# Picking experts for heads 2 to 7 of a prompt tile beside the next tile's first steps

## The reference, cut to what matters

```
q = (xb @ w_query).reshape(blk, 8, 2, 128)              # 8 heads, 2 halves
s = einsum('thcd,ckd->thck', q, sub_keys)               # 128 scores per half
top_s, top_i = top_k(s, 16)
cand = top_s[:, :, 0, :, None] + top_s[:, :, 1, None, :]
best_s, best_j = top_k(cand.reshape(blk, 8, 256), 16)   # 16 experts a head
idx = take_along_axis(cand_idx, best_j); gate = softmax(best_s)
act = gelu(einsum('td,thkd->thk', xb, expert_u[idx]))
out = einsum('thk,thkd->td', gate * act, expert_v[idx])
```

## Time and profile before

| | us |
|---|---|
| time, median of 3 runs | 2681.64 (2680.01 to 2682.45) |
| span of the profiled execution, first to last instruction | 2677.1 |
| TensorE matmul busy | 1865.1 (70%) |
| VectorE busy | 1581.6 (59%) |
| GpSimd busy | 1332.7 (50%) |
| ScalarE busy | 298.2 (11%) |
| moved by DMA | 859.13 MB, 320 GB/s over the span |

### The profile page before, as it was taken

The page is one execution under the profiler, slowest core; times in us unless marked ns, Lnnn a source line. Parts: engine busy times, 40 slices in busy tenths (PEclk is TensorE's granted clock), DMA queues, the critical chain, the costliest instruction groups (busy, mean ns, idle before and its releaser), DMA issues. The chain is left out here.

```text
span 2677.1 us, 23553 instructions
## 1 busy us (share of the span) xinstructions
PE 1865.1 (70%) x7672; PEld 847.1 (32%) x7672; DVE 1581.6 (59%) x3814; ACT 298.2 (11%) x682; POOL 1332.7 (50%) x1480
## 2 busy tenths in 40 slices
PE   7999889974174666677777576755656647556677
PEld 4477755851170001022333224431113422001112
DVE  2388843569998766742649648797454432833311
ACT  2133311210000000001200102100012100000000
POOL 0011521226566777755655446645555444577772
PEclk9999889987556666688898787976778878699999
DMA  4231225439999999999999999998999989999995
GB/s 147 95 126 64 86 56 188 158 112 396 400 400 409 409 409 409 410 374 401 370 405 403 358 392 361 405 402 297 397 366 352 329 316 393 376 409 409 409 408 230
DMA packets 325769, 859.13 MB, mean 321 GB/s; under 512 B 26826, under 2 KB 93338, under 8 KB 325618
## 3 DMA queue, kind: packets, MB, share of 16 engines
q0 software_dynamic: 184320, 671.17, 64.0%
q1 hardware_dynamic: 141326, 186.46, 20.0%
HBM read 845.25 MB, written 12.17 MB: 320 GB/s over the span
## 5 line engine op out<-in xcount | busy, mean ns | idle before, releaser
L2096 DVE SCALAR_TENSOR_TENSOR arena<-arena,banks 128x1024 f32<-128x1024 f32 x640 | 762.4, 1219 | 457.0 <-DMA arena<-peer_u,arena 451.2
L1070 PE MATMUL banks<-arena 128*32 128x512 f32 x2560 | 697.3, 719 | 343.5 <-DMA arena<-peer_v,arena 334.0
L2426 POOL DMA_INDIRECT arena<-peer_v,arena x640 | 609.9, 953 | 435.4 <-issue 203.4
L2426 POOL DMA_INDIRECT arena<-peer_u,arena x640 | 608.2, 950 | 405.3 <-issue 193.6
L1070 PEld LDWEIGHTS banks<-arena 128*32 128x32 f32 x2560 | 92.3, 116 | 823.2 <-DMA arena<-peer_v,arena 666.5
L863 PE MATMUL banks<-wring,uT 128*64 128x512 f32 (+3 forms) x512 | 258.5, 655 | 93.3 <-DMA wring<-w_q 35.0
L536 PE MATMUL banks<-cst,arena 128*128 128x128 f32 (+5 forms) x514 | 79.8, 304 | 177.7 <-DVE arena L1979 82.7
L863 PEld LDWEIGHTS banks<-wring,uT 128*64 128x64 f32 (+1 forms) x512 | 89.2, 184 | 267.8 <-issue 203.2
L564 PE MATMUL banks<-wring,uT 128*128 128x512 f32 (+1 forms) x320 | 142.7, 603 | 0.8 <-DVE uT L1912 0.8
L605 PE MATMUL banks<-uT,wring 128*128 128x320 f32 x512 | 139.1, 433 | 0.0
L536 PEld LDWEIGHTS banks<-cst,arena 128*128 128x128 f32 (+5 forms) x514 | 63.3, 157 | 229.0 <-DVE arena L1979 87.2
(11 more groups left out here) (245 smaller groups left out, 1999.6 us busy)
## 6 DMA issues: line engine op xcount, KB each, us to landing
wring<-peer_w_query SPq DMA_DIRECT2D x40, 1024.0 KB, 18.1
wring<-ssm_w_in SPq DMA_DIRECT2D x24, 1024.0 KB, 7.4
wring<-w_q SPq DMA_DIRECT2D x18, 1024.0 KB, 21.1
wring<-ssm_w_out SPq DMA_DIRECT2D x16, 1024.0 KB, 9.4
wring<-ple_w_gate SPq DMA_DIRECT2D x12, 1024.0 KB, 11.8
arena<-peer_u,arena POOLq DMA_INDIRECT x640, 13.5
arena<-peer_v,arena POOLq DMA_INDIRECT x640, 13.2
out_sample_ssm<-arena SPq DMA_DIRECT2D x16, 512.0 KB, 5.5
```

The costliest lines, as they stand in the source:

```text
L1070: mm = pe.matmul(sums(t, at, half), place_of(t, at), rows_buf[:, k, half * 512:(half + 1) * 512], start=at < spots(t), stop=False, skip_gr ...
L2096: dve.scalar_tensor_tensor(rows_buf[:, k, :], rows_buf[:, k, :], 1.0, u_now, ALU.mult, ALU.mult, accum_out=pact[:, n % 2, at:at + 1]).then ...
L2426: pool.indirect_dma_start(rows_buf[:, k, :], None, tables[kind], bass.IndirectOffsetOnAxis(ap=rows, axis=0))\
```

## The change

Of a prompt tile's four quads only quad 0 is picked in `ask(t)`, which now has 19 steps: 7, five for the quad, 7. Quads 1 to 3 and `finish_select` become a generator `ask_rest(t)` of 17 steps. It runs in the next phase beside the chain of the next tile, one of its steps after every second step of that chain. Since quads 2 and 3 are then not picked while scores arrive, their scores get a place of their own (`late_sc`), in columns 1152 to 2175 of `masks`. The mask of the sample attention covers these columns, so its load moves from the head of SyncE's work for tile 2 to just ahead of the loads of cached keys and values, and also waits there until quad 3 of tile 1 is picked.

```diff
-            return 5 + 6 + 5 + 6 + 14 + (14, 21, 38)[t] + 2 + 3 + 5 + (29, 29, 21)[t]
+            return 5 + 6 + 5 + 6 + 14 + (14, 21, 38)[t] + 2 + 3 + 5 + (19, 19, 21)[t]
...
+        late_sc = masks[:, 1152:2176].rearrange("p (q j k) -> p q j k", q=2, j=4)
+        def score_rows(l, q):
+            return (sc if l == 0 or q < 2 else late_sc)[:, q % 2]
...
+        def beside_half(a, b):
+            for i, _ in enumerate(a):
+                if i % 2 == 0:
+                    next(b, None)
+                yield
+            for _ in b:
+                pass
...  (TensorE; ScalarE has the same two edits)
-                for i in range(27 if t < 2 else 0):
+                for i in range(19 if t < 2 else 0):
...
+                    yield
+                if t == 2:
+                    yield from finish_select(1, t)
+
+            def ask_rest(t):
+                for _ in range(15):
                     yield
                 yield from finish_select(1, t)
...  (TensorE, ScalarE and VectorE)
+                elif ph == 2:
+                    yield from chain(0)
                 elif ph < 5:
-                    yield from chain(ph - 2)
+                    yield from beside_half(chain(ph - 2), ask_rest(ph - 3))
...  (SyncE, tile 2)
-                if t == 2:
-                    sp.wait_ge(*full_at(("oT", 1)))
-                    sp.dma_start(masks[:, 768:768 + SCOLS], I["masks"][:, 1152:]).then_inc(*masks_in.mark("S", 16))
...
                 if t == 2:
                     for n in range(3):
                         sp.wait_ge(*full_at((f"wq{t}", n, t)))
+                    sp.wait_ge(*full_at(("oT", 1)))
+                    sp.wait_ge(*dve_done.at(("gate_in", 1, 1, 3)))
+                    sp.dma_start(masks[:, 768:768 + SCOLS], I["masks"][:, 1152:]).then_inc(*masks_in.mark("S", 16))
                     load_cache(0, 0, (1,))
...  (ScalarE)
-                if q >= 2:
+                if q >= 2 and l == 0:
                     act.wait_ge(*dve_done.at(("gate_in", l, t, q - 2)))
+                elif q >= 2:
+                    if t > 0:
+                        act.wait_ge(*dve_done.at(("gate_in", 1, t - 1, q)))
...  (VectorE)
             def ask(t):
                 for _ in range(7 if t < 2 else 9):
                     yield
-                for q in range(HPT[t] // 2):
+                if t < 2:
+                    yield from pick_quad(1, t, 0)
+                    for _ in range(7):
+                        yield
+                else:
+                    for q in range(2):
+                        yield from pick_quad(1, t, q)
+                    yield from finish_select(1, t)
+
+            def ask_rest(t):
+                for q in (1, 2, 3):
                     yield from pick_quad(1, t, q)
                 yield from finish_select(1, t)
```

More of the change, by code:

```diff
@@ L1426, in take_score @@
                     act.wait_ge(*dve_done.at(("gate_in", l0, t0, HPT[t0] // 2 - 1)))
-                freeing(act.activation(sc[:, q % 2, :, :], bank.rearrange("p (j r) -> p j r", j=4), ACT.Copy), ("score", l, t, q))
+                freeing(act.activation(score_rows(l, q), bank.rearrange("p (j r) -> p j r", j=4), ACT.Copy), ("score", l, t, q))
             def take_sub_keys(l):
@@ L1952, in pick_quad @@
                 for c in (0, 2):
-                    top16(*((sc[:, q % 2, i, :], top_v[:, i, :], top_i[:, i, :]) for i in (c, c + 1)))
+                    top16(*((score_rows(l, q)[:, i, :], top_v[:, i, :], top_i[:, i, :]) for i in (c, c + 1)))
                     yield
```

## The result

The changed kernel takes 2650.73 us (median of 4, 2646.65 to 2654.16) against 2680.92 for the kernel before in the same comparison: ratio 0.9891, 95% interval 0.9878 to 0.9904. I had forecast 2677.4 in a range of 2666 to 2690. The direction was my likeliest by a hair, the size was wrong: 30 us instead of 4, outside the range. Run once more beside other kernels it took 2654.27 (0.9904, 0.9885 to 0.9923).

The account below looks back on a forecast made before the run. It took DMA at about 400 GB/s as the bound, with only unfilled time winnable. Terms -7.6 + 0 + 2 + 1.4 = -4.2 us took 2681.6 to 2677.4 us, range 2666 to 2690.

Parts of the forecast that it names:

- What bounds the kernel: Whole kernel: DMA engines busy at about 400 GB/s, fixed bytes per phase; only time they are not full can be won.
- I take 5.0 us, what the change to phase 3 loses: Change to phase 4: loss falls from 12.6 to 5.0 us, a gain of 7.6, bounds 0 and 9.9.
- the 0 for the change to phase 3: Change to phase 3: same relief, a pick step ahead of the norm; 0 net, bounds 2.3 gained and 2 lost.
- The measure of the loss: Lost time from DMA busy share: (1.03 - share)/1.03 times a stretch's length; 12.6 us at the change to phase 4.
- cleanest: Change to phase 2, loses 2.7 us, the least of the phase changes; one rival brought both others down to it.
- The steps of the chain: Front of phase 3: chain shrinks from 96 to 86 steps, so 29 steps span 7 blocks more, 9 us.
- The stand of TensorE before the transpose: End of phase 3: TensorE waits 15.6 us behind VectorE's picks, freeing no v slot; the wait would go.
- The front of phase 3: First 29 steps: VectorE demand 110.6 of 125.5 us, 88%; 2 us lost, bounds 0 and 10.
- Rival D: VectorE bounds the front of phase 3, losing 10 us; 2685, chance 0.13; sign: rotary wait over 27 us.
- The front of phase 4: VectorE demand 103.5 of 137 us, with VectorE 17.4 us early at the same point; no cost.
- The mask: Phase 4, SyncE: mask load now on the chain takes 3.5 us, net 1.4 lost; bounds 2.1 gained, 22 lost.
- GpSimd: Fronts of phases 3 and 4: gathers 0.98 us beside picks against 0.93, at most 8 us issue time; counted as nothing.

Follow-up runs that it names:

- e1: Changed kernel, but ask(t) of a prompt tile keeps 29 steps (ten empty ones follow), so the weight loads end earlier; 2662.96 us (0.9932).
- e10: Kernel before, with only finish_select moved into the front of the next phase, all four quads picked in their own phase; 2683.7 us (1.001).
- e7: Changed kernel, but in phase 4 ask_rest(1) steps after every chain step, and the mask is loaded ahead of the query weights; 2660.61 us (0.9925).
- e3: Changed kernel with the change for tile 1 alone; tile 0 picks all four quads in its own 29 steps; 2657.83 us (0.9916).
- e4: Kernel before with one edit: the sample attention's mask loaded just ahead of the cached keys, after the attention queries; 2685.08 us (1.0018).
- e11: Changed kernel, with cached values of the last sample pair loaded into a free key buffer instead of the value buffer; 2639.99 us (0.9847).
- e6: Changed kernel, but in phase 4 ask_rest(1) starts six chain steps later, so quad 3 of tile 1 is done later; 2661.97 us (0.9935).

## Why the prediction was wrong

*What bounds the kernel* was right: only lost DMA time can be won. One premise was not: a phase does not move a fixed number of bytes, since loads cross from one to the next.

*"I take 5.0 us, what the change to phase 3 loses"* is the step that failed, with the 0 for the change to phase 3. That change was no model of an undisturbed one, as its own VectorE was late with the same picks; I wrote that it had "the same relief" and still booked 0 for it. Measured: 7.5 us gained at it and 17.6 at the other, 25.1 where I had 7.6, and no loss left at either. e1 shows that relief brings 20.2 of these.

*The measure of the loss* failed too. I read it from the DMA share, which counts starved packets as busy: 12.6 us for the change to phase 4, where the rates of the same rows say 17.3, and 5.0 for the change to phase 3, where they say 6.7. Of the 17.5 us between 7.6 and 25.1, leaving a floor accounts for 10.0 and the share for 6.4; 1.1 more came back than these rates say. The 2.7 us of the change to phase 2, my "cleanest", are 4.3 by rate.

*The steps of the chain* I counted only as a cost (7 more blocks in the front). That 19 steps instead of 29 bring the last loads up to the change, I did not see; the pace is worth 4.9 us at the changes in the table and 9 to 12 in the times of e1, where the rotary of phase 3 (1.9 lost instead of 1.9 gained) and the rest of phase 4 (1.7) also differ.

*The stand of TensorE before the transpose*, my visible reason, was a sign (e10). The size came out small for that reason too: I took away a wait where a whole stretch of demand was taken away.

*The front of phase 3:* 110.6 of 125.5 us forecast, 110.8 of 117 measured, and nothing lost; 2 us booked. Rival D did not come: TensorE waits 16.0 us for the rotary, not over 27. The front can be that full because in it each block shares the DMA engines with weights (61 gathers in 117 us). The same held at the old end of phase 3 until the loads had stopped, and in e7 for 68 us. *The front of phase 4:* no cost, as forecast; SyncE did not wait for quad 3.

*The mask:* the time from the first of these issues to VectorE's release was 65.6 us before (1970.1 to 2035.6) and is 69.5 now. That is 3.9 more, near the 3.5 us that I took:

```profile
1937.09 0.34 SPq L1320 DMA_DIRECT2D uT<-masks  x1
```
```profile
2006.61 2.52 DVE L2274 TENSOR_TENSOR arena<-banks,uT 128x512 f32<-128x512 f32 x4 [26.43 <-issue]
```

Whether it reached the end of the kernel, e3 and e4 leave open. The 5 us that phase 4 is longer are no sign of it: they go with the 5.2 MB more that it moves, and at equal bytes 1.1 us are gained from 1860 to 2360 us.

*GpSimd:* 58.00/61 = 0.95 us a gather beside the picks of the front, not over the 0.93 to 0.98 of the earlier trace rows. The Trainium skill (SBUF — State Buffer, on the port shared by VectorE and GpSimd) lets one block the other fully; with VectorE 95% busy beside 61 gathers the trace does not show it.

The 80% range failed because its bounds for the two changes (9.9 and 2.3 us gained) came from the same yardstick and left a floor of 2.7 us at each. The yardstick alone would not have saved it: by rate, with a floor of 4.3 at each, 6.7 + 17.3 - 8.6 = 15.4 us come off 2681.6, which is 2666, its lower end.

## What to carry to other kernels

Where DMA bounds a kernel, read a stretch's loss from its rate against a full stretch with the same mix of pieces, not from the share of busy time. The mix matters: with 512-byte pieces in it, 1971 to 2035.6 us of the kernel before reads 373 GB/s at a share of 1.05, and nothing is missing. Price a dip as wholly removable in one of your rivals until an undisturbed place shows a floor. Put an engine's heavy work beside the weight loads, where fewer blocks pass in each us, and let the last loads run close to the change of phase: the slots bridge a stretch without loads only for as long as they last (here about 18 us). A waiting engine in such a stretch may be a sign: take the wait away alone before you price it.

## What was not expected of the hardware

In starved stretches 4 KB packets took 0.16 us in the median and over 0.7 in the slowest hundredth, so that 347 GB/s showed a share of 0.94. While both queues had work they moved equal numbers of packets whatever the sizes: 2980 and 2981 from 1736 to 1780 us (10.85 MB of gathers, 6.65 of weights), 2825 and 2823 beside 512-byte pieces, which so got 1.40 MB in 30 us beside 10.27 of gathers. Whether the queues take turns packet by packet or several at a time, the counts do not show. Such a stream was worth starting early in e11 (14 us), yet it caught up with most of a late start in e6, where it met fewer gathers.
